# A block compression whose 30 columns move to the stationary side: four 32-column tiles of TensorE and one transpose

## What is computed

```python
def compress_kv(k, pos_emb, w1, w2):
    B, S, G, D = k.shape
    r = NSA_CMP_LEN // NSA_CMP_STRIDE
    sub = k.reshape(B, S // NSA_CMP_STRIDE, NSA_CMP_STRIDE, G, D)
    nc = S // NSA_CMP_STRIDE - r + 1
    blocks = jnp.concatenate([sub[:, j:j + nc] for j in range(r)], axis=2) + pos_emb[:, None, :]
    flat = blocks.transpose(0, 1, 3, 2, 4).reshape(B, nc, G, NSA_CMP_LEN * D)
    return jax.nn.gelu(flat @ w1) @ w2
```

## Time and profile before

| What | Value |
|---|---|
| Median of 3 runs | 2333.57 us (2330.7 to 2337.37) |
| The profiled execution, its own time | 2334.45 us |
| Its span in the trace | 2332.7 us |
| TensorE matmul busy | 2164.7 us, 93% |
| TensorE weight load busy | 1650.0 us, 71% |
| VectorE busy | 811.4 us, 35% |
| ScalarE busy | 668.7 us, 29% |
| Bytes moved | 610.06 MB, 262 GB/s on average |

### The profile page before, as it was taken

One profiled execution on the slowest core, in us unless ns is written; L12 is line 12 of the kernel. 1 busy time (PEld: TensorE's weight loads), 2 busy tenths in 40 slices (PEclk: granted clock), 3 DMA queues, 4 the chain that ended last, 5 costly groups with the idle time before them and its releaser, 6 DMA issues.

```text
span 2332.7 us, 48106 instructions
## 1 busy us (share of the span) xinstructions
PE 2164.7 (93%) x19824; PEld 1650.0 (71%) x19824; DVE 811.4 (35%) x1482; ACT 668.7 (29%) x1151; POOL 70.2 (3%) x122
## 2 busy tenths in 40 slices
PE   7899888998998879998999998989999999999997
PEld 6674545876754449887899897877666676776675
DVE  5541112646411126984566588540000000000002
ACT  4432223454232225554433346430000000000002
POOL 0100000101000002000000200000000000000000
PEclk9999999999999999999999999989999999999999
DMA  7439999622399996433455652418999999999993
GB/s 246 143 113 418 419 419 362 180 79 62 110 419 419 419 381 155 140 109 126 142 184 157 163 178 91 162 38 297 388 373 398 370 378 401 366 380 400 368 385 126
DMA packets 196758, 610.06 MB, mean 262 GB/s; under 512 B 11472, under 2 KB 87072, under 8 KB 163728
## 3 DMA queue, kind: packets, MB, share of 16 engines
q1 hardware_dynamic: 190688, 590.84, 67.7%
q0 software_dynamic: 5248, 13.25, 2.6%
q10 hardware_dynamic: 560, 2.10, 0.2%
HBM read 605.11 MB, written 1.05 MB: 260 GB/s over the span
## 4 chain that ended last, share of the span: by engine, by line
PE 72%; DVE 12%; DMA 9%; ACT 3%; issue 2%; DVEq 1%; SPq 0%; ACTq 0%; POOLq 0%
PE psum L2236 18%; PE psum L2241 12%; DMA weight_ring<-in_moe_w_up_dram 8%; PE psum L1977 7%; PE psum L137 7%; PE psum L138 6%; PE psum L139 6%; PE psum L2008 2%; DVE weight_ring_rounded L116 2%; PE psum L936 1%; DVE h_cf L3156 1%; ACT scores L970 1%; PE psum L2737 1%; PE psum L2017 1%; PE psum L2273 1%
## 5 line engine op out<-in xcount | busy, mean ns | idle before, releaser
L2236 PE MATMUL psum<-weight_ring,weights_high 128*32 128x512 f32 (+2 forms) x4608 | 477.2, 469 | 0.0
L2241 PE MATMUL psum<-weight_ring,weights_high 128*32 128x256 f32 (+1 forms) x2304 | 444.6, 346 | 0.0
L1977 PE MATMUL psum<-weight_ring,scores 128*64 128x256 f32 x2048 | 262.8, 399 | 50.0 <-DMA weight_ring<-in_moe_w_up_dram 28.8
L2241 PEld LDWEIGHTS psum<-weight_ring,weights_high 128*32 128x32 f32 x2304 | 242.3, 110 | 54.6 <-issue 0.8
L1977 PEld LDWEIGHTS psum<-weight_ring,scores 128*64 128x64 f32 x2048 | 151.9, 141 | 160.6 <-issue 111.5
L2236 PEld LDWEIGHTS psum<-weight_ring,weights_high 128*32 128x32 f32 x4608 | 184.3, 110 | 83.7 <-issue 40.3
L2241 PE MATMUL psum<-weight_ring,xT_high 128*32 128x256 f32 x1056 | 232.2, 379 | 0.0
L2236 PE MATMUL psum<-weight_ring,xT_high 128*32 128x256 f32 (+1 forms) x2112 | 231.5, 486 | 0.0
L137 PE MATMUL psum<-xT_high_rounded,weights_high_rounded 128*128 128x256 f32 x768 | 216.8, 282 | 2.2 <-DVE xT_rounded L369 1.4
L139 PE MATMUL psum<-xT_high_rounded,weight_ring_rounded 128*128 128x256 f32 x768 | 216.2, 282 | 0.0
L2345 DVE TENSOR_TENSOR xT<-xT,psum 128x768 f32<-128x768 f32 (+1 forms) x24 | 21.8, 910 | 511.5 <-PE psum L2241 373.2
(11 more groups left out here) (575 smaller groups left out, 3174.7 us busy)
## 6 DMA issues: line engine op xcount, KB each, us to landing
weight_ring<-in_moe_w_down_dram SPq DMA_DIRECT2D x152, 1024.0 KB, 9.2
weight_ring<-in_moe_w_gate_dram SPq DMA_DIRECT2D x128, 1024.0 KB, 9.9
weight_ring<-in_moe_w_up_dram SPq DMA_DIRECT2D x128, 1024.0 KB, 9.4
weight_ring<-in_moe_w_gate_dram SPq DMA_DIRECT2D x32, 768.0 KB, 6.2
weight_ring<-in_moe_w_up_dram SPq DMA_DIRECT2D x32, 768.0 KB, 4.5
weight_ring<-in_w_in_dram SPq DMA_DIRECT2D x20, 1024.0 KB, 8.4
weight_ring<-in_ffn_w_gate_dram SPq DMA_DIRECT2D x11, 1024.0 KB, 5.2
weight_ring<-in_ffn_w_up_dram SPq DMA_DIRECT2D x11, 1024.0 KB, 5.3
```

What stands on the lines that cost most here:

```text
L1977: last = self.c.nc.tensor.matmul(psum[at:at + W, x % 2, 0:CH], self.x[:, x % 2, k, :], w[:, k, :], start=(k == 0), stop=(k == k1 - 1), ski ...
L2236: last = nc.tensor.matmul(psum[32 * q:32 * q + 32, bank + c0 // 512, 0:c1 - c0], slots(q), w[:, c0:c1], start=start, stop=stop, skip_group ...
L2241: last = nc.tensor.matmul(psum[96:P, bank + c0 // 512, at:at + rest], slots(q, True), w[:, main:], start=start and at == 0, stop=stop, ski ...
```

## The change

The stationary and the moving operand change places. The blocks' 30 columns, read as 32, become the stationary operand; each matmul moves the 128 columns of a weight tile and writes 32 partitions of one PSUM bank: blocks now stand in the partitions and hidden units in the columns. The four results (keys and values, two halves each) take the four quarters of the partitions, and for each j four matmuls with four ring tiles follow one another. All four tiles are taken ahead of the first matmul, and the ring's count goes up by four at the end. VectorE copies the 128 x 128 result from PSUM to a new buffer `hid_rows`, TensorE transposes it into bank 1, and ScalarE's gelu reads from there, each quarter's first 30 columns.

```diff
     pair = CMP_LEN // 2
+    hid_rows = sb("hid_rows", [P, P])
+    hid_copied, hid_turned = c.sig("cmp_rows_copied"), c.sig("cmp_rows_turned")
+    hid_copied.up()
     @c.block.tensor
     def _(pe):
         pe.wait_ge(*c.sig("blocks_padded").now())
@@
         pe.wait_ge(*built.at(3))
         pe.wait_ge(*c.sig("results_taken_act").now())
         pe.wait_ge(*c.sig("results_taken_dve").now())
-        for i, name in enumerate(("c_w_ck1", "c_w_cv1")):
+        w1 = []
+        for name in ("c_w_ck1", "c_w_cv1"):
             src = k_tiles(arg[name][0])
-            for m in range(2):
-                w1 = c.ring.take(pe, src[:, :, m * P:(m + 1) * P])
-                for j in range(pair):
-                    first = (i * pair + j) * at_j
-                    last = nc.tensor.matmul(c.psum[:, 2 * i + m, 0:P], w1[:, j, :], block_rows[:, first:first + P],
-                                            start=(j == 0), stop=(j == pair - 1))
-                last.then_inc(c.ring.used, 1)
+            w1 += [c.ring.take(pe, src[:, :, m * P:(m + 1) * P]) for m in range(2)]
+        for j in range(pair):
+            for q, w in enumerate(w1):
+                first = (q // 2 * pair + j) * at_j
+                last = nc.tensor.matmul(c.psum[32 * q:32 * q + 32, 0, 0:P], block_rows[:, first:first + 32], w[:, j, :],
+                                        start=(j == 0), stop=(j == pair - 1))
+        last.then_inc(c.ring.used, 4)
         c.cmp_tile = c.ring.tiles
+        pe.wait_ge(*hid_copied.at(1))
+        nc.tensor.transpose(c.psum[:, 1, 0:P], hid_rows[:, :], c.ident[:, :]).then_inc(*hid_turned.up())
         pe.wait_ge(*squashed.at(1))
@@
     def _(act):
-        act.wait_ge(c.ring.used, c.cmp_tile)
-        nc.scalar.activation(hid[:, :, :], c.psum[:, 0:2, 0:NSA_G * NCMP], ACT.Gelu_apprx_tanh)
+        act.wait_ge(*hid_turned.at(1))
+        made = c.psum[:, 1, 0:P].rearrange("p (q n) -> p q n", n=32)[:, :, 0:NSA_G * NCMP]
+        nc.scalar.activation(hid[:, :, :], made[:, 0:2], ACT.Gelu_apprx_tanh)
         for m in range(2):
             nc.scalar.activation(hid_stack[:, m].rearrange("p g (h n) -> p g h n", n=NCMP),
-                                 c.psum[:, 2 + m, 0:NSA_G * NCMP].rearrange("p (g n) -> p g n", g=NSA_G).unsqueeze(2).broadcast_to(
+                                 made[:, 2 + m].rearrange("p (g n) -> p g n", g=NSA_G).unsqueeze(2).broadcast_to(
                                      [P, NSA_G, NSA_HPG, NCMP]), ACT.Gelu_apprx_tanh)
@@
     @c.block.vector
     def _(dve):
+        dve.wait_ge(c.ring.used, c.cmp_tile)
+        nc.vector.tensor_copy(hid_rows[:, :], c.psum[:, 0, 0:P]).then_inc(hid_copied.sem, 1)
         dve.wait_ge(*c.sig("masks_ready").now())
         dve.wait_ge(*compressed.at(1))
```

## The result

| | before | changed |
|---|---|---|
| Median | 2332.95 us (4 runs, 2330.7 to 2337.37) | 2317.73 us (4 runs, 2317.24 to 2319.28) |
| Ratio | | 0.9942, interval 0.9926 to 0.9957 |
| Profiled execution | 2334.45 us, span 2332.7 | 2319.28 us, span 2317.6 |

The change is faster, by 15 us, where 10 were forecast. Interval and forecast touch: 0.9957 of 2333 is a saving of 10.0 us.

What follows compares the result with a forecast made beforehand. TensorE was taken as the bound, with the compression loop on the path: 3.68 us of matmuls plus 0.82 of turn make 4.5 instead of 14.56, saving 10.05, so the median 2333.57 becomes 2323.5 us; range 2319.5 to 2329.5.

Steps and rivals of the forecast that it cites:

- The bound and the place: Block compression loop: TensorE sets the time, nothing runs beside it, so a microsecond saved there is saved on the path.
- The 64 matmuls: Compression loop: 128 passes in 32 rounds of four column tiles, 0.109 us a round, 3.68 us in all.
- feeding at 60 ns: Rival in the compression loop: TensorE fed only every 60 ns, loop 7.7 us, whole 2327.7 us; chance 14%.
- Four slots instead of one: Compression loop: tiles read four ring slots where the model rows read one; two streams run abreast, four not shown.
- Weight loads that don't overlap: Rival in the compression loop: each load waits for other tiles' matmuls, 128 pairs 49 us, whole 2369 us; chance 3%.
- The turn: Between loop and gelu: VectorE copy, TensorE transpose and hand-overs, new on the path, 0.82 us, bounds 0.6 and 1.3.
- Waiting for four tiles: Ahead of the loop: waiting for four weight tiles rather than one costs nothing, covered by two projection stages ahead.
- the ring's count at once: End of the loop: ring increments come together instead of four times; the later expert loads stay hidden, no cost.
- absorbed by transfers: Rival behind the loop: a transfer or queue not tied to this chain holds the next stage, 2333.6 us; chance 4%.
- The saving, 10.05 us: First matmul to gelu: 14.56 us before, 4.5 after, bringing the median to 2323.5 us.
- The clock: Rival at the score products: clock falls after the gaps, 1.8 us lost, whole 2325.3 us; chance 18%.
- a median may be off by 2: Whole time: the three runs of before lie 6.7 us apart, so a median's error was put at 2 us.

Runs made afterwards that it cites:

- a1: Kernel before the change with its compression loop over 16 values of j cut to 5: median 2320.4 us over 12 runs, ratio 0.9958.
- a2: Changed kernel with 22 matmuls that nobody reads added ahead of its loop: median 2334.4 us over 11 runs, ratio 1.0008.
- a3: Changed kernel with its two loops exchanged, all 16 matmuls of one column tile before the next tile's: median 2329.7 us over 12 runs, ratio 0.9989.
- b4: Changed kernel with all four column tiles moving the same, first ring slot: 2318.9 us in one run, loop 3.73 us.
- c1: Changed kernel without copy and transpose, gelu reading the matmuls' bank directly: 2319.6 us in one run, first matmul to gelu 3.76 us.
- b1: Changed kernel, unedited, timed again: median 2321.0 us over 11 runs, ratio 0.9953 against the kernel before.
- b3: Kernel before the change, moving 32 block columns per matmul instead of 128: 2346.7 us in one run, first matmul to gelu 25.3 us.

## Why the prediction was wrong, point by point

- **The bound and the place**: right. The loop was on the path with nothing beside it, and what was saved in it, or put back, moved the whole by as much within the intervals (9.8 and 11.8 us in a1, 9.7 and 13.6 in a2, 9.2 and 8.9 in a3).
- **The 64 matmuls, 3.68 us**: right, 3.73. The round of four 128-column passes that stood in the last experts' rows held for 32 rounds in succession. The upper end, feeding at 60 ns, is refuted: 128 matmuls and 128 loads went out in 3.4 us, 27 ns a pair. Of the two figures of the Trainium skill ("TensorE: Matmul & The Clock Gate", "Wait — 56ns, not 53.3ns?"), about 62 ns per matmul with decoding in software and a floor near 25 ns, the first doesn't describe these executions and the second isn't contradicted. Four slots instead of one: nothing (b4).
- **Weight loads that don't overlap**: refuted, since 128 loads of 110 ns, 14 us in series, passed within 3.7 us. The rule of the Trainium skill ("TensorE: Matmul & The Clock Gate", "Part 3: Packing small matmuls — row/col tiling") lets a load overlap with running matmuls only in another row group. Here all matmuls use all rows, so the trace disagrees.
- **The turn, 0.82 us**: 0.71 (c1). Copy 0.30 for 0.28, transpose 0.34 for 0.38; the hand-overs were shorter than allowed. The 0.45 us that the prediction reads from the earlier trace rows is TensorE's piece alone; from VectorE's end to its next start it is 0.51.
- **Waiting for four tiles, the ring's count at once**: nothing, as said. The saving was not absorbed by transfers.
- **The saving, 10.05 us** (14.56 - 4.5 is 10.06): in the edited part 10.09.
- **The clock**: the price, 1.8 us, was right: 1.63, in four of six traces. That the gaps make it fall is likely and not shown (four of six with them, none of four without). 18% looks too low a chance.
- **The step that failed** is "so a median may be off by 2", together with the lower end of the range, "the full saving and a median 4 us down". The clock was weighed in one place only, the score products, and as a loss, and the waits for transfers only as what could absorb the saving. But the clock falls 21 to 28 times in each trace, 95 to 132 us at half clock in all. Some come back in all 13 traces (near 95, 160, 324 and 372 us), others come and go. In the profiled pair the gain outside the edited part was 5.0 us. Single executions of the changed kernel spread over 14 us and of before over 18, and a median of four is a draw from that: the result's four gave 2317.7, and 16 give 2320.8. That is inside the range and 2.7 from the forecast; 1.3 of these 2.7 is the starting value, 2333.57 from three runs where 49 give 2332.3. Worked from there the saving is 11.5 us by the medians and 10 by the parts, and the interval of b1, 7.5 to 14.5 us, holds both.

What stays open: whether the result's four were low by chance alone or also by the occasion. They lie within 2.0 us of one another, closer than the spread of b1 suggests. The kernel before, at 2332.95, 2332.2 and 2332.3 us on the three occasions on which it was run several times, speaks for chance. Open too is what held TensorE for 1.29 us behind the landed transfer in before's trace; as b1 has the same gap, it doesn't go with the change.

No version was found that beats the changed kernel: filling the gaps and starting earlier took 2320.4 and 2322.0 against 2321.0.

## What to carry to other kernels

Where a matmul moves few columns that are wanted, make them the stationary operand and put neighbours in the program into different column tiles: side by side is where the gain is (9.2 of 10.8 us of loop here), while moving fewer columns in the old form cost 10.7 us in the one execution of it (b3). Price such an edit from a place in the same trace that already runs the new shape. And for a saving under half a per cent, weigh the spread of single executions before giving a range: the falls of the clock and the waits for transfers land differently in each execution, and four runs don't average that out.

## What was not expected of the hardware

- With 128 weight columns and 32 moved columns per pass, TensorE fell to half clock after 2.5 us of a loop without gaps and stayed there for the remaining 22.8 us (b3, one execution). With 32 weight columns and 128 moved, four tiles wide, or 128 and 128, it kept full clock.
- When the column tile changes, the first four passes of the next tile start between the last ones of the old, so that a loop ordered by tiles took 12.93 us instead of 14.1 (a3).
- Mean granted clock, which differs by 0.001 to 0.008 from execution to execution of one kernel, goes with 1.4 us for each 0.001.
